# First loads on three queues, half loads for four units, token-major input in two pieces, and the first block's transposes after two more units

## The reference

```python
h = rms_norm(x, norm_gain[l])
proj = jnp.einsum('btd,de->bte', h, w_in[l])           # (256, 2048) x (2048, 9296)
qa, ka, va, ga, qb, kb, vb, gb, qi, ki, wi = jnp.split(proj, offsets, axis=-1)
out_a = chunked_relpos_attention(heads(qa), heads(ka), heads(va), rel_bias[l])
out_b = dsa_sparse_attention(heads(qb), heads(kb), heads(vb), qi, ki, wi, slopes)
y = concat([out_a * silu(ga), out_b * silu(gb)])
x = x + jnp.einsum('bte,ed->btd', y, w_out[l])          # (256, 2048) x (2048, 2048)
return rms_norm(x, final_gain)
```

## Time and profile before

| | us |
|---|---|
| median of 3 runs (lowest, highest) | 556.9 (555.86, 557.62) |
| the profiled execution's own time | 555.07 |
| its span, first to last instruction | 552.9 |
| TensorE busy | 538.4 (97%) |
| VectorE busy | 324.2 (59%) |
| ScalarE busy | 254.8 (46%) |
| GpSimd busy | 29.5 (5%) |

### The profile page before, as it was taken

The page is one execution under the profiler, slowest core; times in us unless marked ns, Lnnn a source line. Parts: engine busy times, 40 slices in busy tenths (PEclk is TensorE's granted clock), DMA queues, the critical chain, the costliest instruction groups (busy, mean ns, idle before and its releaser), DMA issues.

```text
span 552.9 us, 7916 instructions
## 1 busy us (share of the span) xinstructions
PE 538.4 (97%) x2536; PEld 447.2 (81%) x2536; DVE 324.2 (59%) x461; ACT 254.8 (46%) x353; POOL 29.5 (5%) x40
## 2 busy tenths in 40 slices
PE   7998999999999999999999999999999999999994
PEld 4877888888888888888888888888888888888883
DVE  5845456656565566666565555466565648556464
ACT  6774444444444444434544434443544445554332
POOL 1000220202000000000010101010100000000000
PEclk9999999999999999999999999999999999999998
DMA  8966555456655556555544454454554566565613
GB/s 282 420 258 206 175 163 191 149 183 209 208 162 183 189 196 194 198 195 163 191 152 152 161 176 156 156 167 144 188 168 165 167 203 238 191 193 180 207 67 152
DMA packets 28863, 103.65 MB, mean 187 GB/s; under 512 B 3360, under 2 KB 3760, under 8 KB 28464
## 3 DMA queue, kind: packets, MB, share of 16 engines
q1 hardware_dynamic: 27936, 96.82, 52.4%
q0 software_dynamic: 768, 6.31, 3.2%
q10 hardware_dynamic: 144, 0.33, 0.2%
HBM read 101.34 MB, written 2.11 MB: 187 GB/s over the span
## 4 chain that ended last, share of the span: by engine, by line
PE 91%; DMA 4%; DVE 1%; ACT 1%; issue 1%; SPq 1%; DVEq 0%; ACTq 0%
PE acc L342 27%; PE acc L344 27%; PE acc L343 27%; DMA v<-x 2%; PE aux L370 2%; PE aux L490 1%; PE aux L466 1%; DMA qk<-xT 1%; DMA w_raw<-w_blocks 1%; PE aux L405 1%; PE aux L435 1%; DVE w_lo L803 1%; PE aux L494 1%; PE aux L469 1%; PE aux L479 1%
## 5 line engine op out<-in xcount | busy, mean ns | idle before, releaser
L803 DVE TENSOR_TENSOR w_lo<-w_raw,w_hi 128x1024 fp32r<-128x1024 f32 x174 | 215.6, 1240 | 193.7 <-ACT w_hi L583 193.5
L583 ACT ACTIVATE w_hi<-w_raw 128x1024 fp32r<-128x1024 f32 x174 | 184.4, 1060 | 253.9 <-PE acc L344 248.7
L342 PE MATMUL acc<-w_hi,a_hi 128*128 128x512 f32 x704 | 278.4, 395 | 2.1 <-DVE w_lo L803 1.1
L344 PE MATMUL acc<-w_hi,a_lo 128*128 128x512 f32 x704 | 274.4, 390 | 0.0
L343 PE MATMUL acc<-w_lo,a_hi 128*128 128x512 f32 x704 | 274.3, 390 | 0.0
L342 PEld LDWEIGHTS acc<-w_hi,a_hi 128*128 128x128 f32 x704 | 132.3, 188 | 30.7 <-issue 3.5
L344 PEld LDWEIGHTS acc<-w_hi,a_lo 128*128 128x128 f32 x704 | 132.2, 188 | 28.1
L343 PEld LDWEIGHTS acc<-w_lo,a_hi 128*128 128x128 f32 x704 | 132.4, 188 | 25.8
L315 POOL TENSOR_TENSOR q_now<-qk,qscale 128x512 f32<-128x512 f32 x8 | 12.0, 1501 | 271.0 <-PE aux L469 233.3
L693 ACT ACTIVATE p<-p,neg_max 128x256 f32<-128x256 f32 (+1 forms) x32 | 14.1, 442 | 0.7 <-DVE neg_max L982 0.7
L370 PE MATMUL aux<-ident,stage 128*128 128x128 f32 x80 | 10.4, 272 | 2.6 <-DVE stage L811 2.6
(11 more groups left out here) (121 smaller groups left out, 263.3 us busy)
## 6 DMA issues: line engine op xcount, KB each, us to landing
w_raw<-w_blocks SPq DMA_DIRECT2D x142, 512.0 KB, 3.3
w_raw<-wo_blocks SPq DMA_DIRECT2D x32, 512.0 KB, 3.7
v<-x POOLq DMA_DIRECT2D x2, 2048.0 KB, 9.9
qk<-xT SPq DMA_DIRECT2D x7, 256.0 KB, 6.7
w_raw<-w_blocks SPq DMA_DIRECT2D x4, 256.0 KB, 4.2
o<-ext_dram POOLq DMA_DIRECT2D x1, 1024.0 KB, 6.7
fgain<-final_gain POOLq DMA_DIRECT2D x1, 1024.0 KB, 6.7
out<-o SPq DMA_DIRECT2D x2, 512.0 KB, 3.0
```

Of the source, the lines that this page charges most:

```text
L342: nc.tensor.matmul(dst, a_hi[:, k, t], hi, start=start, stop=False)
L344: return nc.tensor.matmul(dst, a_lo[:, k, t], hi, start=False, stop=stop)
L583: nc.scalar.activation(flat(w_hi[:, s, :, :]), w_raw[:, s, :], ACT.Copy).then_inc(hi_done, 1)
L803: nc.vector.tensor_tensor(flat(w_lo[:, s, :, :]), w_raw[:, s, :], flat(w_hi[:, s, :, :]).bitcast(f32), ALU.subtract).then_inc(lo_done, 1)
```

## The change

- SP no longer issues gain and xT tile 0. GpSimd issues gain as its first load, ScalarE issues xT tile 0 before its first table load. SP begins with the first half of the weights.
- Four units instead of two are loaded, split and multiplied in halves. Inside the loop for the later units of block 0, weights now come before the next xT pair.
- VectorE instead of GpSimd fills ki_bd with zeros; the two warm-up products have 448 columns instead of 512. VectorE makes a_hi of k=0. The copy that extends the bias row moves behind the halved units.
- k=0 is multiplied in another order: both token tiles of a_hi x w_hi, then a_lo x w_hi, then a_hi x w_lo, each after its own wait.
- x is loaded in two pieces of 1 MB, a token tile each, by SP, behind the weights of units 1 and 2 of block 1; each square waits for its own piece.
- The narrow product moves ahead of unit 4 of block 1; its transposes and the transposes of block 0 move behind unit 5. ScalarE and VectorE copy their results in that order.
- GpSimd's load of the bias windows into o waits for the squares too, which use the tensor o as a target.

```diff
-HALVED = 2
+HALVED = 4
@@ SP
-            sp.dma_start(gain[:, :], norm_gain).then_inc(gain_landed, 16)
-            sp.dma_start(xT_land[:, 0, :], xT[:, 0, :]).then_inc(xT0_landed, 16)
             for u in range(HALVED):
...
             for u in range(HALVED, UNITS):
-                if u > HALVED:
-                    k = slice(UK * u, UK * u + UK)
-                    sp.dma_start(xT_land[:, k, :], xT[:, k, :]).then_inc(xT_landed[u], 16)
-                if u >= RING:
-                    sp.wait_ge(lo_done, u - RING + 1)
+                sp.wait_ge(lo_done, u - RING + 1)
                 load(u, w_blocks[0, u, :, :])
+                if u + 1 < UNITS:
+                    k = slice(UK * (u + 1), UK * (u + 2))
+                    sp.dma_start(xT_land[:, k, :], xT[:, k, :]).then_inc(xT_landed[u + 1], 16)
             sp.dma_start(nw_raw[:, :], w_narrow).then_inc(nw_landed, 16)
-            with sp.Fori(1, G_OUT) as g:
+            for u in range(UNITS):
+                sp.wait_ge(lo_done, UNITS + (u - RING + 1))
+                load(u, w_blocks[1, u, :, :])
+                if 1 <= u < 1 + TM:
+                    sp.dma_start(x_nat[:, u - 1, :], x[:, u - 1, :]).then_inc(x_landed[u - 1], 16)
+            with sp.Fori(2, G_OUT) as g:
@@ GpSimd
+            pool.dma_start(gain[:, :], norm_gain).then_inc(gain_landed, 16)
             pool.dma_start(bias_ext[:, 0:2 * MAX_REL + 1], rel_bias).then_inc(row_landed, 16)
-            nc.gpsimd.memset(ki_bd[:, :, :], 0.0).then_inc(cleared, 1)
...
-            pool.wait_ge(xT_landed[UNITS - 1], 16)
-            pool.dma_start(x_nat, x).then_inc(x_landed, 16)
...
             pool.wait_ge(ext_stored, 16)
+            pool.wait_ge(ssq_done, TM)
@@ TensorE
-            pe.wait_ge(cleared, 1)
+            zeros = flat(ki_bd[:, :, :])[:, 0:CB - HD // 2]
+            pe.wait_ge(zeroed, 1)
...
+            def first_k(a, w, start):
+                for m in range(TM):
+                    nc.tensor.matmul(acc[:, m * CB:m * CB + CB], a[:, 0, m * P:m * P + P], w[:, 0, 0, :],
+                                     start=start, stop=False)
+
+            pe.wait_ge(a0_done, 1)
+            pe.wait_ge(half_hi, 1)
+            first_k(a_hi, w_hi, True)
+            pe.wait_ge(alo_done, 1)
+            first_k(a_lo, w_hi, False)
+            pe.wait_ge(half_lo, 1)
+            first_k(a_hi, w_lo, False)
...
             for u in range(1, 4):
                 unit(1, u)
-            pe.wait_ge(patterned, 1)
-            transposes(0, 0, None)
-            unit(1, 4)
-            unit(1, 5)
...
             last.then_inc(narrow_done, 1)
-            unit(1, 6)
+            unit(1, 4)
+            unit(1, 5)
+            pe.wait_ge(patterned, 1)
             pe.wait_ge(aux_read[0], 1)
-            pe.wait_ge(var_done, 1)
...
+            transposes(0, 0, None)
+            unit(1, 6)
             unit(1, 7)
@@ ScalarE
+            act.dma_start(xT_land[:, 0, :], xT[:, 0, :]).then_inc(xT0_landed, 16)
             nc.scalar.preload_act_table(ACT.Exp)
-            act.wait_ge(gain_landed, 16)
...
-            act.wait_ge(x_landed, 16)
             for m in range(TM):
+                act.wait_ge(x_landed[m], 16)
...
-            first_half_out(0, qiT[:, 0, :])
+            act.wait_ge(narrow_done, 1)
+            nc.scalar.activation(narrow[:, :], aux[0][0:NARROW, 0:T], ACT.Copy).then_inc(aux_read[0], 1)
             split_hi(0, 16)
             split_hi(0, 17)
-            act.wait_ge(narrow_done, 1)
-            nc.scalar.activation(narrow[:, :], aux[0][0:NARROW, 0:T], ACT.Copy).then_inc(aux_read[0], 1)
+            first_half_out(0, qiT[:, 0, :])
@@ VectorE
-            dve.wait_ge(row_landed, 16)
-            last_bias = bias_ext[:, 2 * MAX_REL:2 * MAX_REL + 1]
-            nc.vector.tensor_copy(bias_ext[:, 2 * MAX_REL + 1:3 * P],
-                                  last_bias.broadcast_to((HEADS, P - 1))).then_inc(ext_ready, 1)
+            nc.vector.memset(ki_bd[:, :, :], 0.0).then_inc(zeroed, 1)
             dve.wait_ge(gain_landed, 16)
+            dve.wait_ge(xT0_landed, 16)
+            nc.vector.tensor_scalar(a_hi[:, 0, :], xT_land[:, 0, :], gain[:, 0:1], None, ALU.mult).then_inc(a0_done, 1)
...
-            second_half_out(0, qiT[:, 1, :])
             split_lo(0, 16)
             split_lo(0, 17)
...
+            second_half_out(0, qiT[:, 1, :])
             split_lo(0, 18)
```

More of the change, by code:

```diff
@@ L142, in hybrid_block @@
         out_landed = sem("out_landed")
+        zeroed = sem("zeroed")
         cleared = sem("cleared")
         patterned = sem("patterned")
+        a0_done = sem("a0_done")
         ahi_done = sem("ahi_done")
@@ L150, in hybrid_block @@
         nlo_done = sem("nlo_done")
-        x_landed = sem("x_landed")
+        x_landed = [sem(f"x_landed{m}") for m in range(TM)]
         ssq_done = sem("ssq_done")
@@ L382, in _ @@
                     k = u * UK + kk
+                    if k == 0:
+                        continue
                     pe.wait_ge(alo_done, k + 1)
@@ L839, in _ @@
                                             ALU.subtract).then_inc((half_lo, lo_done)[kk], 1)
+            dve.wait_ge(row_landed, 16)
+            last_bias = bias_ext[:, 2 * MAX_REL:2 * MAX_REL + 1]
+            nc.vector.tensor_copy(bias_ext[:, 2 * MAX_REL + 1:3 * P],
+                                  last_bias.broadcast_to((HEADS, P - 1))).then_inc(ext_ready, 1)
             for u in range(HALVED, UNITS):
```

25 lines of the change are left out of this document (15 added, 10 removed).

## The result

The changed kernel took 549.99 us (median of 4 runs, 549.58 to 550.61), the kernel before beside it 556.88 (555.86 to 557.62). The ratio is 0.9891, with an interval of 0.9874 to 0.9908. That is 1.9 under the forecast of 551.9, and 0.4 under the lower end of its range. The profiled executions tell another size: 555.07 before, 549.58 after, 5.5 apart, where the forecast for the trace was 5.0.

What follows compares the result with a forecast made beforehand. TensorE's own stream bounds the kernel, with nearly all waits in the first 45 us. 1.5 + 0.5 + 2.85, with two restarts fewer, make 5.0; taken from the median 556.9 this gives 551.9, range 550.4 to 553.9.

Steps and rivals of the forecast that it cites:

- The landmark: The two transposes of ki_nat on TensorE, at 62.04 before; forecast near 57.
- The sum of the trace: Gains 1.5, 0.5 and 2.85, plus two restarts fewer, make 5.0 off the profiled execution: 555.07 to 550.1.
- rival (a): First 12 products run at the lower clock level, 2.7 more; 1.6 of the gain lost, 553.5; chance 0.15.
- The start: First loads and products: landings 0.7 earlier, first product near 5.4, unit 2 at 11.6, gain 1.9 so far.
- The price I took, 0: Gain loaded by GpSimd's queue: nothing lost, since weights come last; 1 us later would cost about 0.3.
- unit 4 0.4 too late: First block: unit 4 ready at 17.5 but due at 17.1, 0.4 lost (0 to 0.8), net gain 1.5.
- The 0.5 goes: Wait before unit 2 of the second block vanishes with x in pieces; 1.4 of slack at the next place.
- the 2.85: Time lost before the first block's transposes, which goes when they move two units later, due at 50.3.
- (b): Stream shifts by the full 0.92, waits at k=2 and unit 4 vanish: 0.8 more gain, 551.1; chance 0.13.
- (c): Halves slow the early stream to 220 GB/s, making unit 4 later by 1.2: 553.1; chance 0.07.
- (d): First piece of x lands no earlier than the whole, 31.6; unit 2 is 2.0 late: 553.9; chance 0.06.
- (e): Slower: second piece of x holds up its queue, slack ends with a landing at 32.3; 558.6 and up; chance 0.02.

Runs made afterwards that it cites:

- The wait filled with work: Kernel before plus three unused products of zeros ahead of the wait of block 0's transposes: 555.60 us, ratio 0.9974.
- the start alone: Kernel before with only first loads on three queues, four units in halves, zeros by VectorE and the new k=0 order: 555.93 us, ratio 0.9985.
- early transposes: Changed kernel with block 0's transposes put back behind unit 3 of block 1: 551.79 us, ratio 0.9921.

## Why the prediction was right, and where it failed

**The outcome.** Faster was right, and so were the places of the gain; the median lies 0.4 below the range.

**The landmark.** Forecast near 57, measured 56.76 and 57.2. The sum of the trace was 5.0; the two traces give 5.3 at the landmark and 5.5 over the whole execution. The profiled execution was forecast at 550.1; it took 549.58, and the median is 549.99.

**The step that failed** is the last of the sum: "The median of the runs is 556.9, 1.8 above it, and I carry the gain over". It takes the 1.8 for scatter that stays. Most of it was a part of what the change removes: in 48 of its 74 executions the kernel before lies in the upper group, and in the trace that we have of that group it loses TensorE's clock in the wait for stage and pays 1.5 for it. The wait filled with work shows it without any other change. With that wait gone the changed kernel has no upper group, and its median lies at what the sum gave for the trace. Of the miss of 1.9, 1.4 is the distance from the lower group, near 555.5, to the median of 556.9, and the other 0.5 is what the gain between the two traces, 5.5, has over the sum of 5.0. The failed step rests on a sentence in rival (a), "the wait of 2.6 before 44.36 did not lower it". That was true of the one execution that was profiled; the same wait of 2.66 did lower it in the next one. The page of the profile could not show this. A spread of 555.86 to 557.62 in the runs, with the profiled one, 555.07, 0.8 below the lowest, might have: it was read as scatter of some 0.7.

**The start: the first product came out nearly right, by luck, and the rest 0.4 short.** Weights landed 1.2 earlier, not 0.7. The kernel with gain and xT on SP has the old order of that queue and had the half at 4.82, where before it was 5.41: so 0.6 of the 1.2 is the queue, and the other 0.6 differs between traces with the same order (4.81, 4.94 and 5.10 in the other traces of the old start). But gain by GpSimd was in at 5.17, not near 3.73. "gain now comes by GpSimd's queue; the nearest row is bias_ext" took that row as it stood, although the change puts 256 KB of weights ahead of everything on SP's queue. The same bias_ext load, first on GpSimd's queue at the same moment, took 2.4 to land in the kernel before and 3.8 with the weights first (gain on ScalarE's queue); with gain and xT tile 0 back at the head of SP's queue in the changed kernel it took 2.6:

```profile
bias_ext<-rel_bias POOLq DMA_DIRECT2D x1, 8.0 KB, 2.4
```

```profile
bias_ext<-rel_bias POOLq DMA_DIRECT2D x1, 8.0 KB, 3.8
```

So the first product started at 5.57 (forecast 5.4), for another reason than forecast. The price I took, 0, is borne out by the trace: ScalarE had w_hi of k=1 at 6.91, so with gain in early w_lo could have begun hardly before the 6.95 at which it did. k=1 started at 7.79 (7.1), because its weights landed at 6.28, and unit 2 at 11.99 (11.6); the start is worth 1.5 up to here, forecast 1.9.

**The halves: "unit 4 0.4 too late" did not come.** In the first trace unit 4 landed at 14.37, not 15.2, and started without a wait. In the second it landed at 15.33, about as forecast:

```profile
15.33 1.06 ACT L599 ACTIVATE w_hi<-w_raw 128x1024 fp32r<-128x1024 f32 x1 [0.28 <-DMA w_raw<-w_blocks]
```

Its w_lo was done at 17.66 there, and TensorE came to it at 17.80, because it had started unit 2 at 12.36 and not at 11.6. So the stall was escaped by 0.1 in one trace and by 0.7 in the other. The 0.4 for the halves was reckoned from the rates of two stretches, 355 against 417; in 8 to 12 us the traces with halves moved 373 to 404 GB/s and those with whole units 377 to 406, which shows no such price. The batching rule of the Trainium skill that the prediction weighed (DMA: Bandwidth & Descriptors, Bandwidth) cost nothing that these traces show. So the net of 1.5 came out as forecast by luck in part, made of 1.5 and nothing, not of 1.9 less 0.4.

**x in two pieces.** Landings were forecast at 27.0 and 30.9 and seen at 26.89 and 31.69; the wait at unit 2 is gone. Unit 3 had 0.6 of slack, not 1.4. As a part by itself, though, "The 0.5 goes" tells only half: without the pieces x lands at 31.7, and the wait there takes most of what the start gains. The two together are worth the 2.0 of the sum; the start alone was worth 0.9, and added to the late transposes it was worth 0.7 by the medians (551.93 with x whole, 552.63 for late transposes alone, run on two chips).

**The transposes.** Forecast at 50.3, measured at 50.40, with no wait; nw_lo was done at 38.0, as forecast. On the kernel before the move alone is worth 2.8 against the lower group, as the 2.85 said, and 4.7 in the median.

**The rivals.** (a) was half right: the clock does matter here, but in the wait of the kernel before and as a gain of the change. At the start the lower level does come in some traces: until about 10 with early transposes and with gain on SP, until 15.88 with xT tile 1 on ScalarE's queue, for the first products with two units in halves and with the start alone. Its "2.7 more" for 12 products is 12 x (0.43 - 0.227) = 2.4 by the prediction's own numbers, and was 2.5 in the one trace where twelve behind a wait ran at that level. Leaving the warm-up out costs nothing that can be measured. (b) and (c) are answered by the landings and by 352 GB/s, (d) and (e) by the first square at 26.89 and the second at 31.69 (27.76 and 32.08 in the second trace), under the 32.3 where the slack was to end. What stays open is why the clock falls in some executions and not in the others. A late x is not the reason: with the start alone the transposes began at 43.93, earlier than in the first trace of before, and it fell.

## What to carry to other kernels

Look at how the single runs lie before carrying a gain from one trace to the median: if they form two groups, ask which wait could make the difference, and fill it with unused work to find out. A wait of a few microseconds on TensorE costs more than its length in the executions in which the clock falls behind it. Time won ahead of a transfer that hardly moves with it is waited away there, so parts that free the start and parts that bring the next landing forward are to be priced together.

## What the runs showed of the hardware

- Behind waits of 2.66 and 2.59 us TensorE's granted clock was 0.50, in the first case until about 49, at a price of 1.5; in the profiled execution before, a wait of 2.60 left it at 1.00. If the upper group of run times is the one with the fall, as the two traces and the filled wait say, it comes in 48 of 74 executions.
- The granted clock reads 1.00 in the first microseconds although products of 512 columns are 0.43 apart (0.23 at the upper level), in 9 to 10 us with early transposes and up to 15.88 with xT tile 1 on ScalarE's queue.
- An 8 KB load at the start took 1.8 to land on SP's queue, 2.9 on ScalarE's and 3.9 on GpSimd's. These are three kernels with different traffic beside it: on GpSimd's queue alone it took 2.4 in the kernel before and 3.8 to 3.9 with the weights first on SP's. The second of these rows is from the run with gain on ScalarE's queue; the third is the changed kernel's (issue, count, KB, us to landing):

```profile
gain<-norm_gain POOLq DMA_DIRECT2D x1, 8.0 KB, 3.9
```

- A load of 128 KB on ScalarE's queue, beside SP's stream, landed after 3.7 as the first there and after 7.0 as the third; on SP's queue it took 3.4.
